# Loading each streamed weight unit as two halves, each with its own semaphore, in a one-core fp32 kernel of two transformer blocks

## The reference, cut to what matters

```python
def expert_choice_ffn(h, w_router, w_gate, w_up, w_down):
    B, n, D = h.shape
    cap = max(1, EC_CAPACITY * n // N_EXPERTS)          # 32 tokens for each expert
    aff = jax.nn.softmax(jnp.einsum("bnd,de->bne", h, w_router).astype(jnp.float32), axis=-1)
    sel_w, sel_idx = lax.top_k(jnp.swapaxes(aff, 1, 2), cap)
    xs = jax.vmap(lambda hb, ib: hb[ib])(h, sel_idx)
    a = jnp.einsum("becd,edf->becf", xs, w_gate)         # three 1024 x 1024 matrices
    u = jnp.einsum("becd,edf->becf", xs, w_up)           # for each of 16 experts
    y = jnp.einsum("becf,efd->becd", jax.nn.silu(a) * u, w_down) * sel_w[..., None]
    scatter = lambda yb, ib: jnp.zeros((n, D), h.dtype).at[ib.reshape(-1)].add(yb.reshape(-1, D))
    return jax.vmap(scatter)(y, sel_idx)
```

## Time and profile before

| | us |
|---|---|
| median of 3 runs | 3236.38 (3227.24 to 3237.57) |
| the profiled execution's own time | 3237.14 |
| its span, first to last instruction | 3235.3 |
| outside the span | 1.8 |
| expert layer 0 (from 697 to 1210) | 513 |
| expert layer 1 (from 1570 to 2092) | 522 |
| TensorE busy | 2789.7 (86%) |
| VectorE busy | 857.7 (27%) |
| ScalarE busy | 343.4 (11%) |

### The profile page before, as it was taken

How to read it: one execution, slowest core, us unless ns; L and a number is a source line. 1 busy time by engine, 2 the same in 40 slices (tenths; PEclk the granted TensorE clock), 3 DMA queues, 4 the chain that set the end, 5 groups by cost and what they waited for, 6 DMA issues and landing times.

```text
span 3235.3 us, 39538 instructions
## 1 busy us (share of the span) xinstructions
PE 2789.7 (86%) x16456; PEld 2008.6 (62%) x16456; DVE 857.7 (27%) x1758; ACT 343.4 (11%) x697; POOL 39.7 (1%) x70
## 2 busy tenths in 40 slices
PE   5999999978888878999555555699999999999998
PEld 2554454455655556788433323487888887888887
DVE  1222321141222234331310101389322102212200
ACT  0011210020000001121100000101210001111000
POOL 1000000000000001000000000000000000000000
PEclk9999999989999999999888778899999999999999
DMA  8433135129999992223599999743333343233341
GB/s 299 169 146 141 64 139 193 65 114 421 397 372 421 406 378 85 91 98 130 211 400 404 372 411 400 324 151 110 117 118 117 143 156 117 104 130 117 136 151 39
DMA packets 95644, 676.19 MB, mean 209 GB/s; under 512 B 11136, under 2 KB 12288, under 8 KB 15232
## 3 DMA queue, kind: packets, MB, share of 16 engines
q1 hardware_dynamic: 91488, 660.17, 52.0%
q0 software_dynamic: 4000, 13.64, 1.4%
HBM read 672.71 MB, written 1.05 MB: 208 GB/s over the span
## 4 chain that ended last, share of the span: by engine, by line
PE 73%; DMA 19%; DVE 3%; issue 2%; SPq 1%; ACT 1%; ACTq 0%; DVEq 0%
PE ps L557 28%; DMA ring<-units 19%; PE ps L817 10%; PE ps L937 9%; PE ps L842 2%; PE ps L1190 2%; PE ps L995 2%; PE ps L1026 2%; PE ps L575 2%; PE ps L646 1%; PE ps L642 1%; PE ps L971 1%; PE ps L566 1%; SPq L467 1%; PE ps L766 1%
## 5 line engine op out<-in xcount | busy, mean ns | idle before, releaser
L937 PE MATMUL ps<-ring,arena 128*64 128x256 f32 (+1 forms) x6144 | 597.0, 437 | 265.0 <-DMA ring<-units 241.5
L937 PEld LDWEIGHTS ps<-ring,arena 128*64 128x64 f32 (+1 forms) x6144 | 372.3, 139 | 473.6 <-issue 347.5
L557 PE MATMUL ps<-h,ring 128*128 128x256 f32 (+1 forms) x2240 | 519.8, 394 | 4.9 <-ACT h L1349 4.9
L557 PEld LDWEIGHTS ps<-h,ring 128*128 128x128 f32 x2240 | 428.0, 192 | 94.4 <-issue 37.8
L817 PE MATMUL ps<-u,ring 128*128 128x512 f32 (+1 forms) x1024 | 340.8, 489 | 6.2 <-DMA ring<-units 6.2
L557 PE MATMUL ps<-arena,ring 128*128 128x256 f32 x1408 | 306.6, 379 | 4.7 <-DVE arena L2104 3.4
L557 PEld LDWEIGHTS ps<-arena,ring 128*128 128x128 f32 x1408 | 267.3, 190 | 42.1 <-DVE arena L2104 4.2
L817 PEld LDWEIGHTS ps<-u,ring 128*128 128x128 f32 x1024 | 194.0, 191 | 142.0 <-issue 120.4
L2000 DVE COPY u<-ps 32x512 f32<-32x512 f32 (+1 forms) x128 | 70.8, 553 | 322.6 <-PE ps L937 321.3
L557 PE MATMUL ps<-u,ring 128*128 128x512 f32 (+1 forms) x256 | 87.7, 503 | 12.7 <-DVE u L1677 7.9
L2147 DVE SCALAR_TENSOR_TENSOR arena<-arena,vec 128x256 f32<-128x256 f32 x240 | 97.1, 478 | 0.0
(11 more groups left out here) (313 smaller groups left out, 2449.1 us busy)
## 6 DMA issues: line engine op xcount, KB each, us to landing
ring<-units SPq DMA_DIRECT2D x624, 1024.0 KB, 10.1
arena<-quarters POOLq DMA_DIRECT2D x32, 256.0 KB, 2.9
arena<-neighbours POOLq DMA_DIRECT2D x32, 64.0 KB, 5.7
h<-tokens SPq DMA_DIRECT2D x1, 2048.0 KB, 37.7
arena<-tokens POOLq DMA_DIRECT2D x1, 2048.0 KB, 8.4
con<-constants SPq DMA_DIRECT2D x1, 1712.0 KB, 41.2
h<-memory POOLq DMA_DIRECT2D x1, 1024.0 KB, 5.9
out<-h SPq DMA_DIRECT2D x2, 512.0 KB, 3.3
```

The source lines that it names most:

```text
L557: last = nc.tensor.matmul(ps[:, g + j, 0:n], w[:, kt, j * P:(j + 1) * P], rhs[:, q * KT + kt, 0:n], start=(q == 0 and kt == 0), stop=(q == ...
L937: last = nc.tensor.matmul(ps[j * slots:(j + 1) * slots, bank, lo:lo + UC], lhsT[:, kt, 0:slots], w[j][:, kt, :], start=(kt == 0), stop=(kt ...
```

## The change

Each unit is loaded by two DMAs in place of one: the first half of the contraction (tiles 0 to 3, 1024 floats or 4 KB of every partition) and the second half. The first raises `loaded[s]`, the second a new semaphore `rest_loaded[s]`. Both are issued behind the same wait for a free slot. In `project`, in the two modulation products and in `chunks`, TensorE waits for the first halves ahead of contraction tile 0, and for the second halves ahead of tile 4. Everything else that calls `unit()` waits for both at once. The number of bytes, the order of units, the ring and the point at which a unit is counted as used stay as they were.

```diff
             for s in range(RING):
-                sp.dma_start(ring[:, s, :], units[s]).then_inc(loaded[s], 16)
+                sp.dma_start(ring[:, s, 0:UNIT // 2], units[s][:, 0:UNIT // 2]).then_inc(loaded[s], 16)
+                sp.dma_start(ring[:, s, UNIT // 2:], units[s][:, UNIT // 2:]).then_inc(rest_loaded[s], 16)
...
                     sp.wait_ge(units_used, i * RING + s + 1)
-                    sp.dma_start(ring[:, s, :], units[bass.ds(i * RING + RING + s, 1)]
+                    following = bass.ds(i * RING + RING + s, 1)
+                    sp.dma_start(ring[:, s, 0:UNIT // 2], units[following, :, 0:UNIT // 2]
                                  .rearrange("a p n -> (a p) n")).then_inc(loaded[s], 16)
+                    sp.dma_start(ring[:, s, UNIT // 2:], units[following, :, UNIT // 2:]
+                                 .rearrange("a p n -> (a p) n")).then_inc(rest_loaded[s], 16)
...
-            def unit():
+            def unit(whole=True):
 
                 n = state["unit"]
-                pe_wait_unit(n)
+                pe_wait_unit(n, loaded)
+                if whole:
+                    pe_wait_unit(n, rest_loaded)
...
+            def rest_of_units(n=1):
+                for q in range(n):
+                    pe_wait_unit(state["unit"] - n + q, rest_loaded)
...
                 for q in range(groups):
-                    w = unit()
+                    w = unit(whole=False)
                     for j in range(tiles):
                         for kt in range(KT):
+                            if j == 0 and kt == KT // 2:
+                                rest_of_units()
...
                     def chunks(bank, lo, lhsT):
-                        w = [unit() for _ in range(beside)]
+                        w = [unit(whole=False) for _ in range(beside)]
                         for kt in range(KT):
+                            if kt == KT // 2:
+                                rest_of_units(beside)
```

More of the change, by code:

```diff
@@ L392, in build @@
         loaded = [sem(f"unit_loaded_{s}") for s in range(RING)]
+        rest_loaded = [sem(f"unit_rest_loaded_{s}") for s in range(RING)]
         units_used = sem("units_used")
@@ L509, in _, with pe_wait_unit @@
             state = {"unit": 0, "product": 0}
-            def unit():
+            def unit(whole=True):
                 n = state["unit"]
-                pe_wait_unit(n)
+                pe_wait_unit(n, loaded)
+                if whole:
+                    pe_wait_unit(n, rest_loaded)
                 state["unit"] += 1
                 return ring[:, n % RING, :].rearrange("p (k c) -> p k c", c=UC)
-            def pe_wait_unit(n):
+            def rest_of_units(n=1):
+                for q in range(n):
+                    pe_wait_unit(state["unit"] - n + q, rest_loaded)
+            def pe_wait_unit(n, arrived):
                 value = 16 * (n // RING + 1)
                 if count.turn is None:
-                    pe.wait_ge(loaded[n % RING], value)
+                    pe.wait_ge(arrived[n % RING], value)
                 else:
-                    pe.wait_ge(loaded[n % RING], count.turn * (16 * state["body"] // RING) + value)
+                    pe.wait_ge(arrived[n % RING], count.turn * (16 * state["body"] // RING) + value)
             def loop(times, body, per):
@@ L619, in modulation @@
                 for n in range(2):
-                    w = [unit() for _ in range(4)]
+                    w = [unit(whole=False) for _ in range(4)]
                     for kt in range(KT):
+                        if kt == KT // 2:
+                            rest_of_units(4)
                         for q in range(4):
```

## The result

The changed kernel takes 3260.69 us (median of 4 runs, 3250.16 to 3265.73) against 3234.61 us for the kernel before in the same session: a ratio of 1.0084, 95% interval 1.0062 to 1.0106. It is 20 to 34 us slower. The profiled execution was the fastest of the four, 3250.16 us with a span of 3248.3 us, so its trace shows half of the loss.

A forecast was written before the change was run, and what follows sets the result against it. DMA was taken to pace the two expert layers. Layer 0 +7.7, layer 1 -0.5, the start -0.6 and SyncE's queue +0.5 sum to +7.1 us, giving 3244 us; the 8-in-10 range was 3228 to 3264.

The forecast's parts named there:

- the likeliest case: Whole kernel: the summed terms, +7.1 us, give 3244 us, own range 3237 to 3251, chance 0.55.
- Part 1, the price of halves: Unit loads: 4 KB runs double packets and completions, adding 0.08 us for a unit, 2.57 us in place of 2.49.
- Part 2, the head start: Chunks waiting for DMA: first halves land 1.28 us earlier, which counts only where the stream stops.
- Layer 0: Layer 0's experts: 40 of 48 units paid in each group, +12.8 us, less 5.1 us head start: +7.7 us.
- Layer 1: Layer 1's experts: +14.1 us price, less 12 us of dips and twice 1.3 us: -0.5 us, from -3.5 to +11.5.
- The start and SyncE's queue: First loads: net -0.6 us; extra SyncE issues behind the branches' modulation products: 0.1 us each, +0.5 us, 0 to 2.
- The waits: TensorE's added wait for each unit in `project` and the rest: already met, leaves no gap, costs nothing.
- Dips stay: Rival, layer 1: holes come from new transfers' first packets, so 12 us don't come back; +19.1, 3256 us, chance 0.20.

The follow-up runs named there:

- E1: The changed kernel run again, unaltered, for its time and a second trace: 3262.85 us, ratio 1.0090 to the kernel before.
- E6: The changed kernel, but the host stores each half as one unbroken 512 KB block: 3244.80 us, ratio 1.0033 to the kernel before.
- E4: The kernel before, one transfer for each unit, but the host stores units as two blocks, giving 4 KB runs: 3251.73 us, ratio 1.0056.
- E7: The kernel before, but two units in one transfer with 16 KB runs, issued when both slots are free: 3292.75 us, ratio 1.0172.
- E2: The changed kernel, but TensorE waits for both halves at the unit's start, so no head start: 3294.58 us, ratio 1.0192 to the kernel before.
- E9: The changed kernel with halves in unbroken 512 KB blocks and TensorE waiting for both at the unit's start: 3263.30 us, ratio 1.0090 to the kernel before.
- E8: The changed kernel, but only units in slots 1 and 5 are loaded as halves, others whole: 3227.88 us, ratio 0.9980 to the kernel before.
- E11: The kernel before, with halves only for slots 1 and 5 while layer 1's experts are loaded: 3222.09 us, ratio 0.9975.
- E12: As E11, but the halved units are laid out as two unbroken blocks: 3222.12 us, ratio 0.9967 to the kernel before.
- E10: The changed kernel, but the branches' gate products wait for the second half in their middle: 3250.31 us, ratio 1.0064 to the kernel before.
- E3: The kernel before with whole loads, but TensorE waits on the unit's one semaphore at its start and again mid-unit: 3233.34 us, ratio 1.0002.
- E5: The kernel before, but each unit in two 64-partition transfers of 8 KB runs, both awaited at the unit's start: 4021.53 us, ratio 1.242.

## Why the prediction was right and where it was wrong

The measured 3260.7 us lies in the range (3228 to 3264) and the likeliest side, slower, was named at 0.46. But the likeliest case, 3244 us, is 17 us short, its own range (3237 to 3251), which had a chance of 0.55, was missed, and the loss of 26 us is nearly four times the +7.1 us of the sum. The wide range held by 3 us, and 18 us of the loss (E1 less E6) have a cause that isn't in the prediction: that it held is in part luck. By its steps:

- **Part 1, the price of halves: right.** 0.08 us for a unit was the term; the rate of 409 GB/s was forecast to the digit, E4 shows it with a single transfer, and E7 shows the same price in the other direction.
- **Part 2, the head start: the mechanism right, its size wrong.** It was valued at 5.1 us in layer 0, about 15 us in layer 1 and 1.3 us at the start; E1 and E2 differ by 32 us, E6 and E9 by about 5 to 6 parts in a thousand, 18 us. The waits behind the modulation products were not counted in it.
- **Layer 0: mis-sized, +7.7 for +13.** Here the step that failed is "In each of the four groups the stream stops once ... Eight of the 48 units load in that shadow". I read one group's end, the one at the loop's turn with its 4.57 us stall, and took it for all. From the chain, group 3's next chunk came 15.9 us after its last landing (1064.0 to 1080.0) where group 2's came after 20.5 us. By the trace's DMA records the ring's queue was empty for 7.6 us behind group 2, and for 2.8 and 1.3 us behind groups 1 and 3; behind group 4 nothing more is paced by it. A stop of 1.3 us can't give back 1.9 us, and 48 units are paid in place of 40. In the changed kernel's first trace the three rests are 1.0, 7.2 and 0 us, 3.5 us less in all; 4.1 us (48 units at 0.085) for each of four groups less 3.5 is +13. That the rest behind group 2 hardly shrank goes with the longer scatter there, which widens it again. Why group 3 takes +4.1, though its stream starts behind the longest rest, stays open.
- **Layer 1: right in the first trace, short by the medians.** Forecast -0.5 (to +11.5), traces +3.2 and +9.9. That dips come from late releases was the main guess of the step, and E8, E11 and E12 bear it out. What failed is that the change also makes new dips (E2's row), which the head start has to pay for first. The dips that stay in the kernel before go with the granted clock, which the prediction left out.
- **The start and SyncE's queue: the second failed.** "It costs when a unit is wanted whole at once ... 0.1 us each". It cost up to 3.2 us at one place in E1 (4.8 us of wait for 1.6 us) and E10 takes most of it back. (Four times 0.1 is 0.4, not 0.5; it changes nothing.) The 0.1 us came from SyncE's issue times, as if the second half followed the first through the engines without a gap. The row in E1 shows 3.9 us between their landings.
- **The waits: right**, E3.
- **"Dips stay", the rival nearest to the result (3256 us)**, has the size but not the reason. The cause that was missing in every case is this one: two transfers for one unit that read alternate 4 KB pieces of the same memory. With unbroken blocks (E6) the change costs +11 us, near the forecast +7, and the other 18 us are the layout's. That nearness is in part luck, since layer 0 alone takes +13 us in E6's trace.

What the runs give as a sum, by the ratios (it is bookkeeping: each term holds only in the order in which the steps are taken): short runs +18 us (E4); a second transfer beside them, from its own block, +11 us (E9 less E4); alternating reads in place of blocks, +33 us more (E2 less E9); head start, -33 us of that (E1 less E2). With blocks, the head start takes 18 us off 29 and leaves +11 (E6). Each difference of two ratios is uncertain by 8 to 10 us, so the 11 us is barely clear of nothing.

Open is why alternating reads land late. SyncE's issues block in both layouts, up to 4.6 us in E1 and 4.2 us in E9, so the issue queue isn't the difference:

```profile
L472 SPq DMA_DIRECT2D ring<-units x616: 332/333/4642, 32.9 to 3187.9; - x154
...
L473 SPq DMA_DIRECT2D ring<-units x616: 332/333/4191, 32.4 to 3190.8; - x154
```

(the first of E1, the second of E9). That the two transfers of a unit are at work at the same time is so in both layouts: at the four places behind the modulation products the ring's queue had moved 0.66 to 0.76 MB when the first half landed. But that first half landed 3.8 to 4.0 us after its issue in E1, and 3.2 to 3.4 us in E9. Something in memory is the likely place, but no run measured it.

## What to carry to other kernels

When a stream of transfers is the bound, price a cut of its transfers in packets, from whatever rows have other packet sizes, and then look for each place where the stream stops, one by one: a head start is worth at most the rest of the stop, and where there is no stop it is worth nothing. Cut only the last transfer that a waiting step needs, and only in the stage where the next release would come too late (here 50 units of 624 in halves gave 0.25% to 0.33%, while halves of all lost 0.9%). If a block is cut, lay its pieces out so that each transfer reads unbroken memory.

## What the runs showed of the hardware that I hadn't expected

- Two transfers that read alternate 4 KB pieces of 1 MB (E2) cost 33 us more by the ratios (1.0192 against 1.0090) than two that read a block of 512 KB each (E9), with the same packets. In a burst into an idle queue the second half landed 3.9 us after the first at the worst place of E1.
- Transfers of 64 partitions moved 229 GB/s with all 16 DMA engines at a share of 1.02, against 421 GB/s for 128 partitions with the same 8 KB runs.
- An issue on SyncE in the loop, 0.33 us as a rule, blocked for up to 4.6 us with two transfers of 4 KB runs for each unit (E1) and for up to 3.1 us with one (E4). With two transfers of 8 KB runs (E5) the longest was 1.6 us, in the kernel before 1.49 us. So it goes with the small packets and not with the number of transfers.
